# A two-block transformer kernel: the expert weights loaded in runs of 8 KB

## Chip, cores, metric

One core of one Trainium2 chip. The metric is device time of one execution in microseconds (us). Before the change three runs took 3195.36, 3199.36 and 3201.74 us.

## What is computed

Two blocks follow each other on a sequence of 512 tokens with 1024 features, all in float32. The first (depth 2) mixes tokens with gated linear attention and differential attention and then has a mixture of 32 experts; the second (depth 2) has grouped attention, spatial gating, a convolution and a gated feed-forward. The change lies in the mixture of experts of the first block, cut to what matters:

```python
for l in range(DEPTH):                         # 2
    mod = c_act @ w_ada[l] + b_ada[l]
    sh1, sc1, g1, sh2, sc2, g2 = jnp.split(mod, 6, axis=-1)
    ...
    h = rms_norm(x, norm2_g[l]) * (1.0 + sc2[:, None, :]) + sh2[:, None, :]
    # hier_moe: every token goes to 2 of the 32 experts, with gates
    hu = lax.ragged_dot(xs, w1, sizes)         # w1: [32, 1024, 1024]
    h_gate, h_up = jnp.split(hu, 2, axis=-1)
    ys = lax.ragged_dot(jax.nn.silu(h_gate) * h_up, w2, sizes)   # w2: [32, 512, 1024]
    out = jnp.zeros_like(t).at[tok_s].add(ys * gate)
    x = x + g2[:, None, :] * out
```

A contraction is a sum over rows of the weight matrix; it may run over them in any order, if both factors use the same one.

## The kernel before

The program is written by hand: five instruction streams (SyncE loads weights, GpSimd does small loads, indirect transfers and subtractions, TensorE, VectorE, ScalarE), tied by semaphores. For each layer of the first block there is a stage A (norm, projections, both attentions, router) and an expert stage; then the second block follows. Tiles, rings and waits of stage A come from a table that lists them in order (`order_a`); SyncE issues the loads in the order of `blocks_a`.

**Expert stage.** Every expert has a block of 64 slots for tokens, full or not. For each expert the three matrices of 512 x 1024 (two halves of w1, j = 0 and 1, and w2, j = 2) come from memory, 6 MB in all. Three sets of buffers (w = 0, 1, 2) take them in turn. `expert` (L685) waits for each matrix until TensorE has read the one before in that buffer (`m_set_read`), then issues two loads of 1 MB (L698), each with two chunks k of 128 rows: partition p gets row 128 k + p, so a partition receives two separate rows of 1024 elements (4 KB each).

GpSimd gathers the tokens of an expert (`gather`, L957): partition 64 c + s holds half c (512 features) of the token in slot s. TensorE turns the four 128-column parts (`turn_x`, L1418), and ScalarE (`copy_x`, L2683) copies each half out of PSUM with a scale and a shift per feature: the modulation, whose columns are the bias and scale operands. Then `gate_up` (L1425) multiplies, accumulating over k and j; ScalarE and VectorE make silu times up; `down` (L1442) turns the result (two transposes), multiplies with w2; ScalarE scales by the gate, and GpSimd scatters the rows to `ys_scratch` (`scatter`, L966). TensorE's order per expert is: gate and up of u, turn of the tokens of u + 1, indices of u + 2, down of u. VectorE writes the indices for a scatter (L2123) only when the scatter before has landed; ScalarE and TensorE are behind that. There are 31 experts in a loop unrolled in rounds, and then single blocks for what did not fit.

**Modulation.** In stage A twelve small blocks of `w_ada` make mod in PSUM, which is added up in `T[:, 0]` (`add_ada`). `turn_ada(1, 11)` (L1129, called at L1339 in step 16 of the attention loop of 18 steps) transposes the later two thirds of it into the PSUM tile ("adt", 1), and VectorE's `modulation` (L1829) adds the bias: `mod` has feature 128 k + p in column k of partition p, and `s1[:, 8:16]` (L2007) is (1 + scale) times the norm's gain. The biases and gains come from `prow`, whose rows are parts of 128 features. `link` (L1798) makes VectorE wait for its own last result.

## Time and profile before

| | |
|---|---|
| median of 3 runs | 3199.36 us (3195.36 to 3201.74) |
| profiled execution | 3193.79 us, span 3191.9 us |
| TensorE busy | 2934.5 us, 92% |
| VectorE, ScalarE, GpSimd busy | 1281.3, 1082.1, 1046.2 us |
| moved by the DMA engines | 665.98 MB, mean 209 GB/s |
| expert loads of 1 MB, both layers | 390 (180 + 90 + 60 + 40 + 20 in the table of issues) |
| packets of the hardware queue | 280128, none of 8 KB or more |
| chain that ended last | TensorE 62%, SyncE's queue 21%, DMA 5%, VectorE 4% |

Time runs from the start of the span. The expert stage of layer 0 lies at about 500 to 1000 us, that of layer 1 at about 1490 to 1990 us; stage A lies before each, and the second block takes the rest. A DMA share is the part of the time in which the 16 DMA engines moved packets. "PE" is TensorE, "PEld" its weight loads, "DVE" VectorE, "ACT" ScalarE, "POOL" GpSimd, "SPq" SyncE's queue.

### The profile page before, as it was taken

The page shows a single profiled execution, that of the slowest core. Times are in us where ns is not written, and L with a number is a line of the kernel's source. Part 1 is how long each engine was busy: PE and PEld are TensorE (multiplying, and loading weights), DVE is VectorE, ACT ScalarE, POOL GpSimd, SP SyncE. Part 2 cuts the span into 40 slices and gives each one's busy share as a digit, 9 for nine tenths or more (in the row PEclk, how much of TensorE's full clock was granted, in tenths as well). Part 3 has the DMA queues.
Part 4 walks back from the last instruction along what each step waited for, and adds up shares of the span by engine and source line. Part 5 has one row for each costly group of instructions (what it writes and reads, how often), then busy time and mean ns, then how long its engine had stood idle before and what let it go on. Part 6 is the DMA issues. An engine that isn't in the chain of part 4 may idle for free.

```text
span 3191.9 us, 43608 instructions
## 1 busy us (share of the span) xinstructions
PE 2934.5 (92%) x15073; PEld 1937.7 (61%) x15073; DVE 1281.3 (40%) x2094; ACT 1082.1 (34%) x1796; POOL 1046.2 (33%) x917
## 2 busy tenths in 40 slices
PE   8999997888887999997998787899999999999999
PEld 5776783333224776685333222666888776688877
DVE  5575433111114565633111111445676223557631
ACT  4435422222223335522222221454433233543330
POOL 6322441111112432350111111514554542245543
PEclk8999998999998999998999999999999999999999
DMA  6335349999998324437999999311323241132232
GB/s 244 132 113 179 129 165 363 409 408 409 408 407 332 132 91 164 165 122 304 406 408 409 410 407 381 118 54 53 106 84 84 73 131 52 53 106 85 74 106 66
DMA packets 295224, 665.98 MB, mean 209 GB/s; under 512 B 24043, under 2 KB 118696, under 8 KB 295056
## 3 DMA queue, kind: packets, MB, share of 16 engines
q1 hardware_dynamic: 280128, 638.13, 53.6%
q0 software_dynamic: 14928, 25.63, 2.3%
q8 instruction: 104, 1.70, 0.2%
q14 instruction: 64, 0.52, 0.1%
HBM read 647.89 MB, written 33.03 MB: 213 GB/s over the span
## 4 chain that ended last, share of the span: by engine, by line
PE 62%; SPq 21%; DMA 5%; DVE 4%; issue 4%; ACT 2%; POOL 1%; ACTq 0%; DVEq 0%; POOLq 0%
PE psum L1039 60%; SPq L698 20%; DMA ys_scratch<-s_units,s_put_at 2%; DMA s_ring<-in_w_expert_in 1%; POOL s_parts L905 1%; PE psum L1681 1%; ACT s_parts L2460 1%; DMA h_scratch<-s_units 1%; DVE s_hid_low L2430 1%; PE psum L1297 1%; SPq L718 1%; DMA s_ring<-in_w_in 0%; ACT s_units L2460 0%; ACT s_units L2702 0%; DMA s_units<-h_scratch,s_take_at 0%
## 5 line engine op out<-in xcount | busy, mean ns | idle before, releaser
L1009 POOL TENSOR_TENSOR s_parts<-s_ring,s_parts 128x512 fp32r<-128x512 f32 x368 | 511.6, 1425 | 638.6 <-ACT s_parts L2460 638.6
L1039 PE MATMUL psum<-s_hid_low,s_parts 128*128 128x512 f32 x2752 | 642.6, 390 | 3.7 <-DVE s_hid_low L2430 3.7
L1039 PE MATMUL psum<-s_parts 128*128 128x512 f32 x2320 | 595.1, 403 | 7.5 <-ACT s_parts L2460 3.9
L1039 PEld LDWEIGHTS psum<-s_hid_low,s_parts 128*128 128x128 f32 x2752 | 515.6, 188 | 115.2 <-DVE s_hid_low L2430 7.1
L1039 PE MATMUL psum<-s_ring,s_units 128*64 128x512 f32 x2160 | 511.6, 622 | 63.4 <-DMA s_ring<-in_w_expert_in 35.2
L1039 PEld LDWEIGHTS psum<-s_parts 128*128 128x128 f32 x2320 | 434.7, 190 | 121.5 <-issue 20.2
L905 POOL TENSOR_TENSOR s_parts<-s_ring,s_parts 128x512 fp32r<-128x512 f32 x224 | 302.1, 1384 | 480.3 <-ACT s_parts L2460 480.3
L1039 PE MATMUL psum<-s_units 128*128 (+8 forms) x2056 | 375.9, 441 | 82.0 <-DVE s_gsl L2124 42.6
L1039 PEld LDWEIGHTS psum<-s_ring,s_units 128*64 128x64 f32 x2160 | 152.9, 142 | 386.2 <-issue 290.4
L1039 PEld LDWEIGHTS psum<-s_units 64*128 64x128 f32 (+3 forms) x2056 | 185.4, 174 | 239.8 <-issue 188.7
L2460 ACT ACTIVATE s_parts<-s_ring 128x4096 fp32r<-128x4096 f32 (+2 forms) x80 | 265.7, 3322 | 171.1 <-PE psum L1039 100.5
L1039 PE MATMUL psum<-s_h_low,s_parts 128*128 128x512 f32 x1152 | 293.9, 390 | 0.0
L957 POOL DMA_INDIRECT s_units<-h_scratch,s_take_at x67 | 80.3, 1198 | 644.0 <-DVE s_take_at L2118 613.7
L2123 DVE TENSOR_SCALAR s_put_at<-psum,s_half_row 128x1 int32<-128x1 f32 x62 | 13.5, 218 | 656.7 <-DMA ys_scratch<-s_units,s_put_at 656.7
L1039 PEld LDWEIGHTS psum<-s_h_low,s_parts 128*128 128x128 f32 x1152 | 216.1, 188 | 46.3 <-issue 1.0
L2688 ACT ACTIVATE s_units<-psum,s_mod,s_s 128x64 f32<-128x64 f32 x536 | 165.9, 416 | 39.3 <-PE psum L1422 33.3
L2460 ACT ACTIVATE s_units<-psum 128x512 f32<-128x512 f32 (+1 forms) x168 | 98.3, 603 | 200.0 <-PE psum L1039 189.9
L2866 ACT ACTIVATE s_units<-s_temps,s_par 128x512 f32<-128x512 f32 x88 | 63.6, 723 | 297.4 <-DVE s_temps L2436 297.0
L2695 ACT ACTIVATE s_units<-psum 128x256 f32<-128x256 f32 x65 | 25.0, 384 | 411.1 <-PE psum L1039 411.0
L966 POOL DMA_INDIRECT ys_scratch<-s_units,s_put_at x62 | 63.0, 1017 | 286.7 <-ACT s_units L2702 249.3
L2702 ACT ACTIVATE s_units<-psum,s_gsl 128x512 f32<-128x512 f32 x65 | 44.7, 688 | 264.8 <-PE psum L1039 264.8
L2440 DVE SCALAR_TENSOR_TENSOR s_units<-s_temps,s_par,s_units 128x511 f32<-128x511 f32 x88 | 91.2, 1036 | 74.7 <-ACT s_units L2866 74.7
(426 smaller groups left out, 2958.0 us busy)
## 6 DMA issues: line engine op xcount, KB each, us to landing
s_ring<-in_w_expert_in SPq DMA_DIRECT2D x180, 1024.0 KB, 19.1
s_ring<-in_w_expert_out SPq DMA_DIRECT2D x90, 1024.0 KB, 19.1
s_units<-in_w_expert_in SPq DMA_DIRECT2D x60, 1024.0 KB, 19.4
s_ring<-in_w_in SPq DMA_DIRECT2D x28, 2048.0 KB, 9.2
s_ring<-in_w_ada SPq DMA_DIRECT2D x24, 2048.0 KB, 9.0
s_hT<-in_w_expert_out SPq DMA_DIRECT2D x40, 1024.0 KB, 19.2
s_ring<-in_ffn_w_up SPq DMA_DIRECT2D x40, 1024.0 KB, 6.7
s_ring<-in_ffn_w_down SPq DMA_DIRECT2D x16, 1408.0 KB, 7.0
```

What stands on the lines that cost most here:

```text
L698: sp.dma_start(set_piece(w, j, c), matrix[:, first + 2 * c:first + 2 * c + 2, :]).then_inc(weights_in_m[w][j][c], 16)
L718: sp.dma_start(slot_view(s, k, n), src).then_inc(weights_in_a[s], 16)
L905: ins = pool.tensor_tensor(parts[:, s, cols], ring[:, s, cols], high_of(n)[:, cols].bitcast(F32), ALU.subtract)
L957: pool.indirect_dma_start(out=xs[u % 2], out_offset=None, in_=h2_dram[:, :], in_offset=bass.IndirectOffsetOnAxis(ap=take_at[:, u % 2, 0:1] ...
L966: pool.indirect_dma_start(out=ys_dram[:, :], out_offset=bass.IndirectOffsetOnAxis(ap=put_at[:, u, 0:1], axis=0), in_=ys[u], in_offset=None ...
L1009: ins = pool.tensor_tensor(parts[:, s, cols], ring[:, s, cols], parts[:, 4 + n % 2, cols].bitcast(F32), ALU.subtract)
L1039: return pe.matmul(o, lhsT=lhsT, rhs=rhs, start=start, stop=stop)
L2440: link(ve.scalar_tensor_tensor(out=up_t[:, b, 1:SEQ], in0=o[:, 0:SEQ - 1], scalar=w[0], in1=up_t[:, b, 1:SEQ], op0=ALU.mult, op1=ALU.add))
L2460: return ae.activation(o, i, ACT.Copy) if scale is None else ae.activation(o, i, ACT.Copy, scale=scale)
L2688: ins = ae.activation(xsT[u % 2][:, k, CAP * j:CAP * j + CAP], psum[:, 2, slots], ACT.Identity, bias=mod[:, 24 + f:25 + f], scale=s1[:, 8 ...
L2702: ae.activation(ys[b], psum[:, 5 + b, :], ACT.Copy, scale=gsl[:, b:b + 1]).then_inc(m_ys_made.sem, m_ys_made.more())
L2866: ae.activation(up_t[:, n % 4, :], product[n % 2], ACT.Copy, scale=par[:, col:col + 1]).then_inc(up_centre.sem, up_centre.more())
```

## The change

A load still has two chunks of 128 rows, but the row of chunk k = 2 q + b in partition p is now 256 q + 2 p + b: the two rows of a partition are neighbours in memory and make one run of 8 KB. What meets the weights in the contraction follows: the transposes read every second column, and shift and scale are also made in that order, in a new tile `paired`, by eight small matmuls per layer on TensorE and some small operations on VectorE. The slot number of the single blocks moves into a free column.

```diff
-LINKS = {"A": 178, "B": 81}
+LINKS = {"A": 181, "B": 81}
...
-    slot_token = sb("slot_token", [P, 1])
+    paired = sb("paired", [P, 6, 2, 2])
+    shift_of_pairs, scale_of_pairs = (paired[:, a:a + 2].rearrange("p m q b -> p (m q b)") for a in (0, 2))
...
+    slot_token = U[:, 26, 0:1]
...
-                matrix = kn(inp["w_expert_in" if j < 2 else "w_expert_out"][l, e], 0, D)
-                first = 4 * j if j < 2 else 0
+                matrix = inp["w_expert_in" if j < 2 else "w_expert_out"][l, e].rearrange("(q p b) n -> p q b n", p=P, b=2)
+                first = 2 * j if j < 2 else 0
                 for c in range(2):
-                    sp.dma_start(set_piece(w, j, c), matrix[:, first + 2 * c:first + 2 * c + 2, :]).then_inc(weights_in_m[w][j][c], 16)
+                    sp.dma_start(set_piece(w, j, c), matrix[:, first + c]).then_inc(weights_in_m[w][j][c], 16)
...
                 pe.wait_ge(TA.by(("ada", last)).sem, TA.freed_at(l, ("ada", last)))
+                if half:
+                    for h in range(2):
+                        for b in range(2):
+                            mm(o[64 * h:64 * h + 64, P + P * b:2 * P + P * b], T[:, 0, 0:P].rearrange("p (i b) -> p b i", b=2)[:, b, :], ident[:], True, True)
+                            mm(o[64 * h:64 * h + 64, 384 + 64 * b:448 + 64 * b], prow[0:64, 0, :].rearrange("p (i b) -> p b i", b=2)[:, b, :], ident[0:64, 0:64], True, True)
                 done(pe.transpose(o[:, 0:P], T[:, 0, 0:P], ident[:]))
...
                 for k in range(4):
-                    last = pe.transpose(psum[:, 2, tok(k)], xs[u % 2][:, tok(k)], ident[:])
+                    last = pe.transpose(psum[:, 2, tok(k)], xs[u % 2][:, 256 * (k // 2):256 * (k // 2) + 256].rearrange("p (i b) -> p b i", b=2)[:, k % 2, :], ident[:])
...
                 for k in range(2):
-                    last = pe.transpose(psum[:, 4, tok(k)], act[b][:, tok(k)], ident[:])
+                    last = pe.transpose(psum[:, 4, tok(k)], act[b].rearrange("p (i c) -> p c i", c=2)[:, k, :], ident[:])
...
                 if i == LAST_STEP - 1:
+                    o = done(("adt", 1))
+                    for h in range(2):
+                        half = slice(64 * h, 64 * h + 64)
+                        rows_of = o[half, 384:512].rearrange("p (b m r) -> p m r b", b=2, r=4)
+                        for q in range(2):
+                            ve.tensor_copy(paired[half, 0:4, q, :], rows_of[:, 6:10, 2 * q + h, :])
+                            ins = ve.tensor_copy(paired[half, 4:6, q, :], rows_of[:, 14:16, 2 * q + h, :])
+                    link(ins)
+                    for h in range(2):
+                        half = slice(64 * h, 64 * h + 64)
+                        made_of = o[half, P:384].rearrange("p (b r j) -> p r j b", b=2, r=4)
+                        for q in range(2):
+                            ins = ve.tensor_tensor(paired[half, 0:4, q, :], made_of[:, 2 * q + h, 6:10, :], paired[half, 0:4, q, :], ALU.add)
+                    link(ins)
+                    link(ve.scalar_tensor_tensor(out=scale_of_pairs, in0=scale_of_pairs, scalar=1.0, in1=paired[:, 4:6].rearrange("p m q b -> p (m q b)"), op0=ALU.add, op1=ALU.mult))
                     modulation(1, 4, 12)
...
                         ins = ae.activation(xsT[u % 2][:, k, CAP * j:CAP * j + CAP], psum[:, 2, slots], ACT.Identity,
-                                            bias=mod[:, 24 + f:25 + f], scale=s1[:, 8 + f:9 + f])
+                                            bias=shift_of_pairs[:, f:f + 1], scale=scale_of_pairs[:, f:f + 1])
```

The order of instructions shows two places. SyncE's loads for one matrix of the first set that is loaded, before:

```order
L698 ISA
L698 DMA s_units<-in_w_expert_in 128x2x1024
L698 ISA
L698 DMA s_units<-in_w_expert_in 128x2x1024
```

and now:

```order
L700 ISA
L700 DMA s_units<-in_w_expert_in 128x2048
L700 ISA
L700 DMA s_units<-in_w_expert_in 128x2048
```

Number and place of the loads are as before; the instruction's pattern has one run per partition.

TensorE at the second turn of the modulation (`s_temps` is T, `s_prow` the rows of parameters), before:

```order
L1039 MATMUL psum<-s_hid_low,s_parts 128x512 x4
L1083 REGISTER_ALU
L1132 REGISTER_ALU
L1133 MATMUL psum<-s_ident,s_temps 128x128
L1083 REGISTER_ALU
L1297 MATMUL psum<-s_ident,s_units 128x128 x4
```

and now:

```order
L1041 MATMUL psum<-s_hid_low,s_parts 128x512 x4
L1085 REGISTER_ALU
L1134 REGISTER_ALU
L1041 MATMUL psum<-s_ident,s_temps 64x128
L1041 MATMUL psum<-s_ident,s_prow 64x64
L1041 MATMUL psum<-s_ident,s_temps 64x128
L1041 MATMUL psum<-s_ident,s_prow 64x64
L1041 MATMUL psum<-s_ident,s_temps 64x128
L1041 MATMUL psum<-s_ident,s_prow 64x64
L1041 MATMUL psum<-s_ident,s_temps 64x128
L1041 MATMUL psum<-s_ident,s_prow 64x64
L1140 MATMUL psum<-s_ident,s_temps 128x128
```

Eight small matmuls stand ahead of the transpose, behind the same waits. VectorE has 13 more instructions behind the tile's signal, ahead of L1831 of before.

## Rows read from the trace of the kernel before

**Rows 1.** page, part 2: 40 slices of about 80 us
```profile
GB/s 244 132 113 179 129 165 363 409 408 409 408 407 332 132 91 164 165 122 304 406 408 409 410 407 381 118 54 53 106 84 84 73 131 52 53 106 85 74 106 66
```

**Rows 2.** busy time by windows, in us; the loads at the start, then both expert stages
```profile
core 0: us, PE busy (x) PEld busy (x) DVE busy (x) ACT busy (x) POOL busy (x), PEclk, DMA share, GB/s
4.00:6.00 2.00, 1.09 (x5) 1.09 (x6) 0.00 (x0) 0.00 (x0) 1.65 (x7) 1.00 1.03 408
14.00:20.00 6.00, 6.00 (x9) 2.36 (x8) 0.00 (x0) 2.33 (x3) 3.95 (x34) 0.57 1.05 387
520.00:560.00 40.00, 35.75 (x182) 14.02 (x178) 5.03 (x18) 10.64 (x30) 5.58 (x5) 1.00 1.03 405
560.00:960.00 400.00, 345.30 (x1636) 129.05 (x1632) 48.98 (x156) 97.66 (x265) 58.71 (x53) 0.97 1.03 408
1500.00:1560.00 60.00, 54.27 (x271) 20.99 (x271) 8.50 (x26) 16.12 (x47) 10.01 (x9) 1.00 1.03 406
1560.00:1950.00 390.00, 330.27 (x1572) 122.68 (x1568) 46.70 (x151) 93.70 (x255) 57.10 (x51) 0.97 1.03 408
```

**Rows 3.** SyncE's queue in time, start and length, expert stage of layer 0
```profile
642.41 12.94 SPq L698 DMA_DIRECT2D s_ring<-in_w_expert_in  x4
```

**Rows 4.** DMA queues and issues, 560 to 960 us; median us to landing
```profile
q1 hardware_dynamic: 40392, 155.71, 97.6%
q0 software_dynamic: 4217, 7.45, 5.0%
...
s_ring<-in_w_expert_in SPq DMA_DIRECT2D x66, 1024.0 KB, 19.3
```

**Rows 5.** chain that ended last, 515 to 560 us: start, length
```profile
523.69 5.90 DMA ys_scratch<-s_units,s_put_at
...
537.55 5.93 DMA ys_scratch<-s_units,s_put_at
...
551.38 5.85 DMA ys_scratch<-s_units,s_put_at
```

**Rows 6.** L966, the scatter, expert stage of layer 0, then of layer 1
```profile
L966 POOL DMA_INDIRECT ys_scratch<-s_units,s_put_at x31: 1002/1017/1038, 523.7 to 976.3; - x31
...
L966 POOL DMA_INDIRECT ys_scratch<-s_units,s_put_at x31: 1002/1014/1030, 1506.3 to 1959.9; - x31
```

**Rows 7.** small GpSimd loads, us to landing: first 60 us, then 440 to 520 us
```profile
s_prow<-in_diff_qnorm_g POOLq DMA_DIRECT2D x2, 0.2 KB, 5.0
...
s_prow<-in_diff_qnorm_g POOLq DMA_DIRECT2D x2, 0.2 KB, 1.7
...
s_prow<-in_q_norm_g POOLq DMA_DIRECT2D x2, 0.2 KB, 5.2
```

**Rows 8.** TensorE in time around the second turn of the modulation, layer 0
```profile
342.78 0.62 PE L1039 MATMUL psum<-s_ring,s_cact 128*32 128x128 f32 x16
...
346.59 0.27 PE L1133 MATMUL psum<-s_ident,s_temps 128*128 128x128 f32 x1
346.70 0.60 PE L1297 MATMUL psum<-s_ident,s_units 128*128 128x128 f32 x4
```

**Rows 9.** chain that ended last, 340 to 395 us
```profile
346.75 0.11 PE psum L1133
...
347.30 47.78 PE psum L1039 x196
```

**Rows 10.** VectorE in time at the same place
```profile
347.39 0.18 DVE L1831 TENSOR_TENSOR s_mod<-psum,s_par 128x32 f32<-128x32 f32 x1
347.61 0.17 DVE L2007 SCALAR_TENSOR_TENSOR s_s<-s_mod,s_par 128x8 f32<-128x8 f32 x1
350.09 0.69 DVE L1973 TENSOR_TENSOR s_temps<-psum,s_temps 128x512 f32<-128x512 f32 x1 [2.31 <-PE psum L1039]
```

**Rows 11.** groups by line and form, 560 to 960 us: the transposes of an expert
```profile
L1422 PE MATMUL psum<-s_ident,s_units 128*128 128x128 f32 x104 | 17.1, 287 | 0.0
...
L1447 PE MATMUL psum<-s_ident,s_units 128*128 128x128 f32 x52 | 11.1, 295 | 1.1 <-DVE s_units L2181 1.1
```

More of the change, by code:

```diff
@@ L2130, in write_gate @@
                     ve.wait_ge(m_scattered[1], count * 16 + 32)
-                ve.tensor_copy(slot_token[:], psum[:, 7, 0:1]).then_inc(m_put_written.sem, m_put_written.more())
+                ve.tensor_copy(slot_token, psum[:, 7, 0:1]).then_inc(m_put_written.sem, m_put_written.more())
                 ve.tensor_copy(gsl[:, 1:2], psum[:, 7, 2:3]).then_inc(m_put_written.sem, m_put_written.more())
```

## Prediction

> **What bounds the kernel.** I read the 40 slices first, then windows, then the chain of waits. In the slices [rows 1] the transfer rate stands at 406 to 410 GB/s in two blocks of about 450 us, the expert stages of the two layers, and far below that elsewhere. The windows [rows 2] show the same rate with the 16 DMA engines busy at a share of 1.03 (a share over 1 means that records overlap a little), while TensorE is busy for 345 of 400 us and the other engines for less than a quarter. SyncE's queue has the next set's buffers free and still needs 12.94 us to issue four 1 MB loads [rows 3]: it is held by the full DMA queue. A load lands 19.3 us after its issue [rows 4], although 1 MB takes 2.6 us at 408 GB/s. So from about 520 us and from about 1500 us the DMA engines set the pace.
>
> The chain names something else in the first part of the stage: one scatter after the other, 13.86 us apart, each 5.9 us in flight [rows 5]. That is the speed of the computing side. But the 31 scatters of a stage span 452.6 and 453.6 us [rows 6], 15.1 us apiece. The three weight sets loaded ahead are eaten up first, and then the loads decide. Between the two lie 1.2 us per expert: what a faster transfer can win before the computing side binds.
>
> **The change, part by part.**
>
> *Loads.* Bytes, number of DMAs and buffers stay. The instruction moves rows of 2048 elements instead of 2 x 1024. If the queue turns each into one packet, a load has 128 packets of 8 KB and not 256 of 4 KB. What a packet costs beyond its bytes comes from two saturated windows [rows 2]. At 14 to 20 us the adaptation weights come in runs of 512 elements, 2 KB, at 387 GB/s: 16 x 2048 / 387 = 84.7 ns per packet and engine. In the expert stage, with 4 KB, 408 GB/s give 16 x 4096 / 408 = 160.6 ns. Two small packets less one large one leave 8.8 ns per packet. (The input rows at 4 to 6 us, 4 KB too, also reach 408.) An 8 KB packet should then take 2 x 160.6 - 8.8 = 312.4 ns, or 420 GB/s.
> The queue of these loads moved 155.71 MB in 400 us [rows 4]. Over the 890 us of saturated windows [rows 2] (520 to 960, 1500 to 1950) that is 346 MB, or 346e6 / 16 / 8192 = 2640 pairs per engine. 2640 x 8.8 ns = **23.3 us** less. The first loads of each layer, before 520 us, win nothing: they wait for buffers and for the router. No row has an HBM load of 8 KB from this queue, so the price is bounded: at the low end 0 (no fixed part is saved), at the high end half as much again, 13 ns, 34 us. I take the middle, since two loads from the same queue give it.
>
> *Landing of the small transfers.* Gathers and scatters share the engines with packets twice as long. The nearest rows are tiny GpSimd loads [rows 7]: 1.7 us to landing on an idle queue, 5.0 us behind the 2 KB packets of the first 60 us, 5.2 us for the similar ones issued last, behind the first expert loads of 4 KB. Twice the packet, hardly more wait: what they wait behind is an amount of bytes, not a number of packets. So the scatter's 6 us stay within 0.3 us, and I count 0. The Trainium skill ("DMA: Bandwidth & Descriptors", Queues, rings and completion order) says otherwise: an engine drains a whole packet of about 9 to 17 descriptors from one ring before it turns to the next. By that rule the wait would double with the descriptor; rows 7 do not agree, as it did not double from 2 to 4 KB.
>
> *Transposes.* Four of the input and two of the activation per expert now read every second column. Contiguous ones take 287 and 295 ns [rows 11]. No row has such a stride, so: 0 at the low end, twice the time, 6 x 0.29 = 1.7 us per expert, at the high end. A gain is excluded, as the element count is the same. I take 0, for two reasons: TensorE is not what is waited for after the first experts, and only more than the margin of the computing side (below) could show.
> The Trainium skill ("SBUF — State Buffer", Door 1: The DMA port swizzle) states that accesses keep full bandwidth as long as two fall into one 16-byte line; a stride of two fp32 does just that. No row here shows it, and the sum does not use it.
>
> *TensorE, once per layer.* Eight small matmuls stand before the turn of the modulation, at 346.6 us [rows 8]. TensorE is the chain there and goes on unbroken for 47.78 us [rows 9], so they count in full. Neighbours: 16 matmuls with 128 moving columns in 0.62 us, 0.04 us each; four transposes in 0.60 us, 0.15 us each; a single one 0.27 us [rows 8]. The new ones alternate between two kinds and fill half the array; 8 x 0.15 = 1.2 us, 0.3 to 2.2 us as ends. Two layers: **+2.4 us** (0.6 to 4.4).
>
> *VectorE, once per layer.* Eight copies, four additions, one product, with three waits on its own results. The nearest small ones take 0.18 and 0.17 us, 0.22 us apart [rows 10]; 13 x 0.2 = 2.6 us. Behind them VectorE was idle for 2.31 us, until TensorE's next tile [rows 10], which now comes 1.2 us later. At most 0.3 us of delay is left, and TensorE's run of 47.78 us waits for none of it: 0. Without that cover it would be 2 x 2.6 us. ScalarE reads bias and scale from another tile in the same 8 instructions, and the slot number has another place: 0.
>
> **Sum:** -23.3 + 2.4 = -20.9 us. The profiled execution took 3193.8 us (span 3191.9) and would take 3172.9. It lies 0.17% under the median of the three runs, 3199.4, and against that the forecast is **3178.5 us**, 0.65% less. Its own range runs from -34 + 0.6 to -16 + 4.4: 3166 to 3188 us.
>
> **Rivals.**
> *The computing side takes over (slower).* Twice the packet length could double the wait of a scatter in the engines. Its place is the scatter's landing, which VectorE awaits before it writes the next indices; its own products, TensorE's down part and the next scatter are queued behind that. The price is the loaded part of the flight: 6.0 less the 3 us or so that a transfer needs on its own (1.7 us landing plus 1.0 us of issue in rows 6), so +3 us per expert: 13.86 + 3 = 16.9 us. After the change the loads would need 15.1 - 23.3 / 60 = 14.7 us per expert; so from 0.8 us more on the computing side decides, from 1.2 us more the kernel is slower. At 16.9 us, 60 intervals x 1.8 us: about +108 us, with the 2.4 us 3310 us. The rule of the Trainium skill quoted above would show in this way. For it: 13.86 us is near 15.1, and the chain does run through the scatters. Against it: rows 7. The transposes at their high end would work the same way, 13.86 + 1.7 = 15.6, +0.5 x 60 + 2.4: 3232 us. Together 9%.
> *The rate does not move (the change doesn't do what it says).* The queue may cut at 4 KB, or the 408 GB/s may be a limit of memory or ports that small packets miss for another reason. Only the additions stay: 3199.4 + 2.4 = 3202 us, 0.08% more. For it: every packet of these loads is 4 KB so far, and nothing shows a longer one from this queue. Against it: the rate does depend on the run (387 to 408). 15%.
> *Half the gain.* The rate rises but the computing side, 0.8 us away, meets it in part: 3188 to 3193 us. 6%, in the range.
>
> **Numbers.** Forecast 70%, half the gain 6%, no movement 15%, slower by the computing side 9%. A difference within 0.2% (6.4 us) can't be told from none. Faster: 0.76; same: 0.15; slower: 0.09. The range reaches from the forecast's low end to the case without movement: 3166 to 3202 us.
>
> **What would show it.** Right: packets of the loads' queue fall by 390 x 128 = 49920 (390 expert loads in the profile's table); the windows of the expert stages read 418 to 421 GB/s; 31 scatters span about 441 us; landing of a scatter stays at 6.0 us; the turn of the modulation is some 1.2 us longer on TensorE. SyncE's loads may take longer to land, as more bytes fit into the queue; that alone costs nothing. Wrong: 408 GB/s as before (cut packets or another limit), a share below 1 in the windows with scatters over 7 us in flight (computing side), or transposes at 0.5 us.

## The result and the profile after

The changed kernel takes **3266.76 us** (median of 4 runs, 3253.45 to 3270.57) against 3200.55 us for the kernel before on the same chip (3195.36 to 3203.01, 4 runs): ratio 1.0206, 95% interval [1.0188, 1.0223]. It is 2.1% slower; the forecast was 0.65% faster. The profiled execution took 3270.2 us, span 3268.4. Two of the four runs of rest_4k below (3357.86 and 3369.13 us) fell in a slower state, over 1.5% above the fastest of the same kernel, and are left out of its time.

Line numbers of after are those of before plus 2 (SyncE's loads L700, matmuls L1041, scatter L968), further down plus 7 (turn of the tokens L1429, of the activation L1454) and more (put index L2145, gate column L2146). The 40 slices and the queues of the page:

```profile
PEclk8999997889899999998899899999999999999999
GB/s 238 129 115 189 107 187 354 400 401 402 398 403 260 156 64 161 187 106 264 389 402 391 405 403 289 215 60 52 104 97 58 107 121 59 52 84 97 78 99 69
...
q1 hardware_dynamic: 230208, 638.13, 51.7%
```

The packets fell by 280128 - 230208 = 49920, exactly as forecast, so the chip does use single packets of 8 KB. But the blocks of the expert stages read 389 to 405 GB/s instead of 406 to 410 [rows 1] and last longer. The windows of both stages, to be laid beside [rows 2]:

```profile
560.00:960.00 400.00, 344.05 (x1520) 133.61 (x1518) 45.65 (x144) 90.33 (x245) 53.62 (x49) 0.90 0.98 400
1560.00:1950.00 390.00, 334.36 (x1466) 128.85 (x1468) 44.90 (x140) 86.86 (x236) 52.68 (x48) 0.90 0.98 397
```

TensorE is busy as long as before (344 of 400 us) and gets less done (1520 matmuls, before 1636), since its granted clock is 0.90 instead of 0.97. The DMA share fell from 1.03 to 0.98: the engines are no longer full. The queue says the same. A load lands 8.8 us after its issue, not 19.3 [rows 4], and SyncE's queue is 1% of the chain that ended last, not 21%; TensorE is 70% of it. So **the computing side sets the pace**. Landings in the window 560 to 960 us:

```profile
s_ring<-in_w_expert_in SPq DMA_DIRECT2D x66, 1024.0 KB, 8.8
...
ys_scratch<-s_units,s_put_at POOLq DMA_INDIRECT x25, 6.9
s_units<-h_scratch,s_take_at POOLq DMA_INDIRECT x24, 6.7
```

Before, the scatter took 6.1 us in the same window and the gather 6.3:

```profile
s_units<-h_scratch,s_take_at POOLq DMA_INDIRECT x27, 6.3
ys_scratch<-s_units,s_put_at POOLq DMA_INDIRECT x26, 6.1
```

The same scatters in rows like [rows 6]:

```profile
L968 POOL DMA_INDIRECT ys_scratch<-s_units,s_put_at x31: 1002/1017/1038, 531.6 to 1018.3; - x31
...
L968 POOL DMA_INDIRECT ys_scratch<-s_units,s_put_at x31: 1001/1014/1030, 1552.0 to 2041.1; - x31
```

486.7 and 489.1 us, where before had 452.6 and 453.6: +34.1 and +35.5 us, or 16.2 and 16.3 us per expert for 15.1. That is 69.6 of the 76.5 us by which the spans differ. The rest: the first scatter comes 7.9 us later, the way from the last scatter of layer 0 to the first of layer 1 takes 533.7 us for 530.0, and what follows the last scatter is 4.7 us shorter.

Groups by line and form, 560 to 960 us, show where TensorE stands still and what the new access costs. First the matmuls that make the indices (name of the engine and line, then shapes, count | busy, mean ns | idle before, releaser), then the two kinds of transposes with their weight loads:

```profile
L1041 PE MATMUL psum<-s_units 128*128 x192 | 26.4, 260 | 43.3 <-DVE s_gsl L2146 43.3
...
L1429 PE MATMUL psum<-s_ident,s_units 128*128 128x128 f32 x96 | 17.9, 309 | 0.0
L1429 PEld LDWEIGHTS psum<-s_ident,s_units 128*128 128x128 f32 x96 | 13.3, 207 | 19.5 <-issue 19.5
L1454 PE MATMUL psum<-s_ident,s_units 128*128 128x128 f32 x48 | 11.7, 329 | 0.0
L1454 PEld LDWEIGHTS psum<-s_ident,s_units 128*128 128x128 f32 x48 | 9.5, 247 | 0.0
```

The same groups of before, window as above:

```profile
L1039 PE MATMUL psum<-s_units 128*128 x208 | 26.6, 251 | 20.3 <-DVE s_gsl L2124 20.3
...
L1422 PEld LDWEIGHTS psum<-s_ident,s_units 128*128 128x128 f32 x104 | 10.9, 141 | 21.1 <-issue 21.1
...
L1447 PEld LDWEIGHTS psum<-s_ident,s_units 128*128 128x128 f32 x52 | 7.2, 179 | 1.2 <-DVE s_units L2181 1.2
```

Eight index matmuls belong to an expert, so TensorE waited 43.3 / 24 = 1.8 us per expert for VectorE, which waited for the scatter to land; before it was 20.3 / 26 = 0.8 us. What such a wait does to the clock is seen in windows of 2 us. Here 664 to 676 us of after, first TensorE's two pauses in time (in square brackets: idle before, releaser), then the windows:

```profile
668.50 1.05 PE L1041 MATMUL psum<-s_units 128*128 x8 [2.16 <-DVE s_gsl L2146]
...
670.41 4.06 PE L1041 MATMUL psum<-s_ring,s_units 128*64 128x512 f32 x10 [0.54 <-DVE s_units L2207]
```

```profile
664.00:666.00 2.00, 2.00 (x11) 0.69 (x8) 0.00 (x0) 0.21 (x1) 0.00 (x0) 1.00 1.01 397
666.00:668.00 2.00, 0.34 (x3) 0.15 (x2) 0.00 (x0) 1.80 (x7) 0.00 (x0) 1.00 1.05 440
668.00:670.00 2.00, 1.37 (x10) 1.19 (x10) 0.80 (x5) 0.85 (x3) 0.00 (x0) 1.00 0.96 406
670.00:672.00 2.00, 1.59 (x4) 0.51 (x6) 1.05 (x3) 0.00 (x0) 1.10 (x1) 0.62 1.06 446
672.00:674.00 2.00, 2.00 (x8) 0.64 (x6) 0.00 (x0) 0.00 (x0) 0.24 (x1) 0.53 0.98 414
674.00:676.00 2.00, 2.00 (x12) 0.60 (x10) 0.00 (x0) 0.02 (x1) 0.00 (x0) 1.00 1.01 422
```

TensorE stood still for much of 666 to 670 us; from about 670.5 to 674 it works at half its clock (1.2 of 2.4 GHz) and has 8 large matmuls in 2 us instead of 11 or 12. The half clock begins some 2 us behind the end of the pause for the indices, just behind the second, short pause. That short pause of about 0.5 us ahead of the down part is there in the trace of before too, and in the runs with filler matmuls below, whose clock is 1.00; the long one is what differs. The trace's clock record has 23 such stretches between the first and last scatter of each layer, 89 and 92 us together; before had 8 and 6 (27 and 20 us). An interval between scatters without one takes 14.2 to 14.7 us in layer 0 (the last 12.8), one with it mostly 16 to 17.5. Half the clock for 3.9 us (89 / 23) costs 1.9 us of work, so 23 stretches in 30 intervals cost 1.5 us per expert: an estimate from these figures, and the size of the step from 14.7 to 16.2 us.

Theory A, with which the experiments began (the first expectations call it the packet theory): 8 KB packets make the scatter land later, the longer wait for the scatter takes TensorE's clock down, and the low clock is most of the loss. Its rivals: the strided transposes, the 8 KB packets by themselves, or the order in which the engines wait.

### The profile page after: what moved, and what is told of

Same layout as the page of the kernel before. It is cut to its first block, busy times and chain, and to the rows that moved or that the text cites. A ratio compares the mean times of both kernels' runs of the same rounds, so it can differ in the third digit from the quotient of the medians.

```text
span 3268.4 us, 43706 instructions
## 1 busy us (share of the span) xinstructions
PE 3006.2 (92%) x15105; PEld 1977.7 (61%) x15105; DVE 1286.7 (39%) x2120; ACT 1081.1 (33%) x1796; POOL 1045.6 (32%) x917
## 3 DMA queue, kind: packets, MB, share of 16 engines
q1 hardware_dynamic: 230208, 638.13, 51.7%
## 4 chain that ended last, share of the span: by engine, by line
PE 70%; DMA 14%; DVE 5%; issue 5%; ACT 3%; POOL 1%; SPq 1%; DVEq 0%; ACTq 0%; POOLq 0%
PE psum L1041 68%; DMA ys_scratch<-s_units,s_put_at 12%; ACT s_units L2724 1%; POOL s_parts L907 1%; PE psum L1688 1%; DVE s_units L2207 1%; ACT s_parts L2482 1%; DMA h_scratch<-s_units 1%; DVE s_hid_low L2452 1%; PE psum L1304 1%; SPq L720 1%; PE psum L1454 0%; DMA s_ring<-in_w_in 0%; ACT s_units L2482 0%; DVE s_h_low L1856 0%
## 5 line engine op out<-in xcount | busy, mean ns | idle before, releaser
L1041 PE MATMUL psum<-s_hid_low,s_parts 128*128 128x512 f32 x2752 | 642.7, 390 | 3.7 <-DVE s_hid_low L2452 3.7
L1041 PE MATMUL psum<-s_parts 128*128 128x512 f32 x2320 | 595.9, 404 | 7.5 <-ACT s_parts L2482 3.9
L1041 PEld LDWEIGHTS psum<-s_hid_low,s_parts 128*128 128x128 f32 x2752 | 515.7, 188 | 115.1 <-DVE s_hid_low L2452 7.1
L1041 PE MATMUL psum<-s_ring,s_units 128*64 128x512 f32 x2160 | 541.5, 659 | 27.1 <-DVE s_units L2207 23.7
L1041 PEld LDWEIGHTS psum<-s_parts 128*128 128x128 f32 x2320 | 435.3, 191 | 121.3 <-issue 18.1
L1041 PE MATMUL psum<-s_units 128*128 (+8 forms) x2056 | 375.2, 441 | 126.0 <-DVE s_gsl L2146 106.0
L1041 PEld LDWEIGHTS psum<-s_ring,s_units 128*64 128x64 f32 x2160 | 165.0, 151 | 367.5 <-issue 333.8
L1041 PEld LDWEIGHTS psum<-s_units 64*128 64x128 f32 (+3 forms) x2056 | 188.4, 176 | 279.4 <-issue 253.7
L2145 DVE TENSOR_SCALAR s_put_at<-psum,s_half_row 128x1 int32<-128x1 f32 x62 | 13.5, 218 | 766.6 <-DMA ys_scratch<-s_units,s_put_at 766.6
L1041 PE MATMUL psum<-s_h_low,s_parts 128*128 128x512 f32 x1152 | 293.9, 390 | 0.0
L1041 PEld LDWEIGHTS psum<-s_h_low,s_parts 128*128 128x128 f32 x1152 | 216.2, 188 | 46.0 <-issue 1.0
L2710 ACT ACTIVATE s_units<-psum,s_paired 128x64 f32<-128x64 f32 x536 | 165.4, 415 | 43.5 <-PE psum L1429 42.8
L968 POOL DMA_INDIRECT ys_scratch<-s_units,s_put_at x62 | 63.0, 1017 | 345.3 <-ACT s_units L2724 300.6
```

The source lines that it names most:

```text
L968: pool.indirect_dma_start(out=ys_dram[:, :], out_offset=bass.IndirectOffsetOnAxis(ap=put_at[:, u, 0:1], axis=0), in_=ys[u], in_offset=None ...
L1041: return pe.matmul(o, lhsT=lhsT, rhs=rhs, start=start, stop=stop)
L2710: ins = ae.activation(xsT[u % 2][:, k, CAP * j:CAP * j + CAP], psum[:, 2, slots], ACT.Identity, bias=shift_of_pairs[:, f:f + 1], scale=sca ...
```

## The experiments

All were timed in 3 or 5 rounds beside the kernel before on the same chip (medians of 3195 to 3198 us), and the ratios are to that; the row "after" is the result above, to its 3200.55 us. The factors, one by one:

| run | packets | transposes | added | median us | ratio [95%] | layer 0: 31 scatters, us; clock, GB/s 560:960 |
|---|---|---|---|---|---|---|
| before | 4 KB | contiguous | - | 3195 to 3198 | 1 | 452.6; 0.97, 408 |
| after | 8 KB | strided | - | 3266.76 | 1.0206 [1.0188, 1.0223] | 486.7; 0.90, 400 |
| strided_4k | 4 KB | strided | - | 3179.60 | 0.9949 [0.9932, 0.9966] | 452.4; 0.96, 408 |
| loads_8k | 8 KB | contiguous | - | 3226.49 | 1.0101 [1.0074, 1.0128] | 485.7; 0.92, 405 |
| fill_8k | 8 KB | strided | 8 matmuls | 3186.98 | 0.9957 [0.9937, 0.9977] | 444.1; 1.00, 419 |
| fill_8k_again | 8 KB | strided | 8 matmuls | 3190.06 | 0.9975 [0.9962, 0.9988] | 443.0; 1.00, 420 |
| fill_loads_8k | 8 KB | contiguous | 8 matmuls | 3148.61 | 0.9849 [0.983, 0.9867] | 440.9; 1.00, 420 |
| fill_4k | 4 KB | contiguous | 8 matmuls | 3199.81 | 1.0015 [1.0003, 1.0026] | 451.9; 1.00, 408 |
| delay_4k_b | 4 KB | contiguous | 6 copies | 3201.75 | 1.0016 [1.0002, 1.003] | 454.2; 0.94, 408 |
| delay12_4k | 4 KB | contiguous | 12 copies | 3256.17 | 1.0171 [1.0145, 1.0196] | 486.7; 0.91, 401 |

strided_4k, loads_8k and fill_loads_8k multiply columns with the wrong rows. The second layer then routes otherwise and moves 659.7 MB in all, not 666.0, which is one expert's 6.3 MB or about 15 us at 408 GB/s. Their whole times are lower by that, so they are compared in layer 0.

### Which part does it

**rest_4k**: the change with 4 KB packets; load c takes row b = c of both q, so that the rows a load reads lie 8 KB apart in memory, and TensorE needs the second load of a matrix before its second chunk and not before its third.

```diff
-                    sp.dma_start(set_piece(w, j, c), matrix[:, first + c]).then_inc(weights_in_m[w][j][c], 16)
+                    sp.dma_start(set_piece(w, j, c), matrix[:, first:first + 2, c]).then_inc(weights_in_m[w][j][c], 16)
...
-                        if k % 2 == 0:
-                            pe.wait_ge(weights_in_m[w][j][k // 2], used * 16 + 16)
+                        if k < 2:
+                            pe.wait_ge(weights_in_m[w][j][k], used * 16 + 16)
...
```

> All of the change but the packet: each load takes one row of each pair, 4 KB, from two blocks of 256 rows; strided transposes, the added matmuls and VectorE operations stay. Packet theory (8 KB packets hold up the scatters, TensorE then waits longer and its clock falls once per expert): the slowdown goes, 3203 to 3212 us (3200.6 plus 2 x 2.7 us of additions in stage A), scatters 15.1 to 15.3 us apart, landing 6.0 us, granted clock of the expert stage 0.97. Stride theory (the transposes that read every second column cost the computing side its margin): stays at 3240 to 3270 us.

Measured: 3269.65 and 3286.60 us, no better than the change itself and, by the number alone, where the stride theory had it. Layer 0 kept 15.2 us per expert (408 GB/s, clock 0.92), layer 1 took 17.3 us (378 GB/s, clock 0.89). In layer 1, 1560 to 1950 us, the scatter lands latest of all runs, with 4 KB packets:

```profile
ys_scratch<-s_units,s_put_at POOLq DMA_INDIRECT x22, 7.7
```

```profile
L1041 PE MATMUL psum<-s_units 128*128 x184 | 25.9, 263 | 57.9 <-DVE s_gsl L2146 57.9
```

That is 57.9 / 23 = 2.5 us of wait per expert and 29 half-clock stretches in 30 intervals. The chain that ended last runs there through the scatter (46% of 1640 to 1740 us), and TensorE's only waits from 1560 to 1950 us are these 57.9 us and 11.6 us for VectorE ahead of the down part, none for weights. So this run agrees with the second half of theory A, in that the late scatter goes with a long wait and a low clock; but the size of a packet is not all that makes a scatter late. What did it here (the order of the rows in memory is one candidate) was not tested. The run does not answer its own question, so the stride needed strided_4k below.

**loads_8k**: only the load's pattern of the diff, transposes and the rest as before.

> The reverse: the kernel before with loads of 8 KB runs alone; transposes and modulation stay in the old order, so weights meet the wrong columns, and the routing of layer 1 may differ (layer 0's does not). Packet theory: slow, layer 0's 31 scatters some 16.0 to 16.5 us apart, landing 6.9 us, clock near 0.90; in all 3240 to 3265 us. Stride theory: fast, 3177 to 3190 us, scatters 14.7 us apart.

Measured, layer 0:

```profile
L966 POOL DMA_INDIRECT ys_scratch<-s_units,s_put_at x31: 1003/1021/1042, 529.4 to 1015.1; - x31
```

485.7 us for 31 scatters, as slow as the change (486.7), at a clock of 0.92, with 47.6 us of wait before the indices and the scatter landing after 6.9 us. **In layer 0 the 8 KB packets alone cause the loss.** In layer 1, which routes otherwise here, the same loads took 463.9 us, with 16 half-clock stretches and a landing of 6.6 us: slower than before too, by less.

**strided_4k**: the change with the loads and waits of before, word for word.

```diff
-                matrix = inp["w_expert_in" if j < 2 else "w_expert_out"][l, e].rearrange("(q p b) n -> p q b n", p=P, b=2)
-                first = 2 * j if j < 2 else 0
+                matrix = kn(inp["w_expert_in" if j < 2 else "w_expert_out"][l, e], 0, D)
+                first = 4 * j if j < 2 else 0
                 for c in range(2):
-                    sp.dma_start(set_piece(w, j, c), matrix[:, first + c]).then_inc(weights_in_m[w][j][c], 16)
+                    sp.dma_start(set_piece(w, j, c), matrix[:, first + 2 * c:first + 2 * c + 2, :]).then_inc(weights_in_m[w][j][c], 16)
```

> The change with the loads of before, word for word: 4 KB packets of neighbouring rows, and the waits of before, with strided transposes, paired shift and scale and the additions of the first stage. It leaves out that weights and columns agree, so it multiplies wrong pairs; the second layer routes by them, so only the first layer's expert stage is compared. Theory A (a matmul that reads every second column, 22 and 34 ns longer and with weight loads of 207 and 247 in place of 141 and 179 ns, costs the clock by itself): window 560:960 at a clock of 0.90 to 0.93, scatters over 15.6 us apart, 3215 to 3270 us. Theory C (the clock was lost in the earlier 4 KB run through its waiting for both pieces): clock 0.97, scatters 15.1 us apart, 3205 us (3195 plus 5.4 for the additions, plus or minus 5).

Measured: as theory C expected of the stride. The stage takes 452.4 us (before 452.6) at 408 GB/s, though the transposes are those that take longer:

```profile
L1429 PE MATMUL psum<-s_ident,s_units 128*128 128x128 f32 x108 | 20.1, 308 | 0.0
...
L1454 PE MATMUL psum<-s_ident,s_units 128*128 128x128 f32 x54 | 12.9, 323 | 1.0 <-DVE s_units L2203 1.0
```

The stride costs 21 ns and 28 ns per transpose [rows 11], some 0.15 us per expert, hidden under the loads. There are 11 and 10 half-clock stretches where before had 8 and 6. Theory C's reason for the slow rest_4k, its waits for both loads, is not borne out: its trace shows the late scatter above.

### Is it the clock

**fill_8k**, and **fill_8k_again**: the changed kernel with eight idle matmuls where TensorE would wait for the indices; their output is read by nobody.

```diff
+                    for _ in range(8):
+                        mm(psum[:, 3, 0:P], ident[:], ident[:], True, True)
                     indices(number + ROUND * g, ROUND * g + (u + 2), u + 2)
```

> The changed kernel with 8 idle matmuls of 128 columns per expert into an unused PSUM bank, placed where TensorE waits for the scatter's landing (between the turn of the tokens and the indices). If the falling clock is a part of the loss: clock back to 0.95 or more in the expert stage, scatters 14.8 to 15.3 us apart, 3185 to 3225 us. If the clock only follows and the late landing alone costs the time: no gain, 3260 to 3290 us, as TensorE's work only grows by about 1.2 us per expert.

> The changed kernel with the same eight idle matmuls once more, beside the one with 4 KB packets. Theory A: again 0.3 to 0.6% faster than before, 3178 to 3192 us, 418 GB/s in the expert stage, scatters 14.8 to 15.1 us apart, and faster than the 4 KB version with eight matmuls. Theory B: equal to that version.

Measured: 3186.98 and 3190.06 us, faster than before both times, if by less than half a per cent. The windows of fill_8k_again:

```profile
560.00:960.00 400.00, 385.15 (x2120) 185.63 (x2118) 50.44 (x161) 100.96 (x275) 59.09 (x55) 1.00 1.01 420
1560.00:1950.00 390.00, 372.99 (x2038) 179.06 (x2038) 50.77 (x161) 99.17 (x272) 57.33 (x52) 0.99 1.01 419
```

and TensorE in time in fill_8k, 652.8 to 657 us (the eight stand as 16 records, in two passes, and take 1.95 us):

```profile
652.79 0.74 PE L1429 MATMUL psum<-s_ident,s_units 128*128 128x128 f32 x4
653.37 1.95 PE L1041 MATMUL psum<-s_ident 128*128 128x128 f32 x16
655.16 1.05 PE L1041 MATMUL psum<-s_units 128*128 x8
```

The long pause is gone, the clock is at 1.00, and the 8 KB packets deliver the 420 GB/s that the prediction had worked out. TensorE does more work and the kernel is 77 to 80 us faster than the change. The cure is not complete in every trace: in layer 1 of fill_8k four half-clock stretches (17 us) remain, and the 31 scatters take 453.1 us there, as before the change. The Trainium skill ("TensorE: Matmul & The Clock Gate", A second HAM failure mode: psum-queue depth-cycling) tells of a kernel in which short pauses between groups of matmuls make the clock oscillate. The trace of after agrees: in layer 0 the pauses ahead of its half-clock stretches are 1.15 to 2.9 us long.

**fill_4k**: the kernel before with the same eight.

> The kernel before, 4 KB packets and contiguous transposes, with eight idle 128-column matmuls ahead of the indices of each expert. It separates what the eight matmuls give from what the 8 KB packets give. Theory A (the matmuls only mend a clock that the changed kernel had lost; before, the queue of the loads set the pace at a granted clock of 0.97): the DMA share stays 1.03 at 408 GB/s in the window 560:960, the 31 scatters stay 15.1 us apart, time 3195 +- 4 us, no difference. Theory B (the matmuls help any version by the same amount, and the 8 KB packets give nothing): scatters 14.8 us apart, about 3183 us, as much as the changed kernel with the same eight.

Measured: 451.9 us for the stage, 408 GB/s, clock 1.00, 3199.81 us, ratio 1.0015: theory A, 0.8 us above its range. A full clock gives nothing where the loads set the pace; the gain of fill_8k is that of the packets.

**fill_loads_8k**: loads_8k with the eight.

> The kernel before with 8 KB packets alone, contiguous transposes and no additions, and eight idle matmuls ahead of the indices. It multiplies wrong pairs, so only the first layer's expert stage is compared. Theory A (with the clock kept up, 8 KB packets give what the packet count says and the stride costs little): clock 0.98 or more, 418 to 420 GB/s, scatters 14.7 to 14.9 us apart, as in the changed kernel with eight matmuls (14.80). Theory D (the stride still costs 0.3 us or more per expert when the clock is kept up): scatters 0.3 us or more closer than 14.80.

Measured: 14.7 us per expert in both layers, 420 and 417 GB/s. With strided transposes layer 0 took 14.8 (443.0 and 444.1 us for 440.9), so the stride costs about 0.1 us per expert here, not 0.3: theory A.

**reorder_8k**: down(u) ahead of the indices of u + 2 on TensorE, the activation's product ahead of the indices on VectorE, scatter ahead of gather on GpSimd.

```diff
-                    indices(number + ROUND * g, ROUND * g + (u + 2), u + 2)
                     down(made + ROUND * g, used[w] + (2 * g + u // SETS), u, w)
+                    indices(number + ROUND * g, ROUND * g + (u + 2), u + 2)
...
-                    write_put(number + 2 * g, counts[1 - u] + (g + u), u + 1)
                     multiply(made + 2 * g, u)
-                    write_take(number + 2 * g, taken[u] + g, u + 2)
                     turned_act(made + 2 * g, u)
+                    write_put(number + 2 * g, counts[1 - u] + (g + u), u + 1)
+                    write_take(number + 2 * g, taken[u] + g, u + 2)
...
-                    gather(number + 2 * g, u + 2)
                     scatter(made + 2 * g, number + 2 * g, u)
+                    gather(number + 2 * g, u + 2)
```

> The changed kernel with the wait for the scatter taken out of TensorE's way: TensorE does the down part of an expert before the indices of the one after next, VectorE writes the indices for the scatter after its two products, and GpSimd issues the scatter before the gather. Packet theory: the scatter has 4 us more to land, the computing side needs about 14 us per expert and the loads decide at 420 GB/s: 3180 to 3200 us, clock 0.95 or more. Stride theory: little changes, as the transposes are still there: 3240 us or more.

Measured: 3289.13 us, ratio 1.029 [1.0269, 1.0312], clock 0.91. A miss: the wait went away before the indices and came back before the tokens, longer (52.1 / 24 = 2.2 us per expert):

```profile
L1041 PE MATMUL psum<-s_units 128*128 x199 | 26.3, 255 | 0.0
...
L1429 PE MATMUL psum<-s_ident,s_units 128*128 128x128 f32 x96 | 21.1, 353 | 52.1 <-DMA s_units<-h_scratch,s_take_at 52.1
```

### Is a wait enough, without 8 KB packets

**delay_4k_b**: the kernel before with six one-column copies on VectorE behind the scatter's landing; **delay12_4k** with twelve (the scratch columns of half width).

```diff
                 ve.wait_ge(m_scattered[u % 2], count * 16 + 32)
+                for i in range(6):
+                    ve.tensor_copy(spare[:, u % 2, i:i + 1], psum[:, 7, 1:2])
                 ve.tensor_scalar(put_at[:, u % 2, :], psum[:, 7, 1:2], 2.0, half_row[:, 0:1], ALU.mult, ALU.add).then_inc(m_put_written.sem, m_put_written.more())
```

> The kernel before, word for word in its loads and transposes, with six one-column copies on VectorE between the scatter's landing and the next put indices, about 6 x 0.14 = 0.85 us per expert: as much as the scatter's landing grew with 8 KB packets. Theory A (TensorE's wait for the indices, when it grows by nearly a microsecond, takes the granted clock down, and that is most of the loss): computing side at 13.86 + 0.85 = 14.7 us before the clock answers, then over 15.6 us between scatters, clock 0.90 to 0.93 in the window 560:960, DMA share under 1.0, 3225 to 3265 us, without a single 8 KB packet. Theory E (8 KB packets lower the clock or slow the kernel in another way, a wait alone does not): 14.7 us is under the loads' pace of 15.1 us, so scatters stay 15.1 us apart at 0.97 and the time 3197 +- 4 us.

Measured: between the theories. Wait and clock moved as A says, the time did not:

```profile
L1040 PE MATMUL psum<-s_units 128*128 x215 | 28.8, 257 | 37.0 <-DVE s_gsl L2127 37.0
```

```profile
560.00:960.00 400.00, 348.13 (x1629) 133.52 (x1630) 58.63 (x314) 97.91 (x268) 58.34 (x53) 0.94 1.03 408
```

1.4 us of wait per expert (37.0 / 27), 13 stretches at half clock in a layer; the intervals alternate between about 14.2 and 16.0 us and average 15.1, which is what the loads need anyway. The kernel had slack for nearly half of its experts at the low clock. What A had missed is this slack. The delay was also smaller than meant. VectorE in time, for this run and for the one with twelve:

```profile
650.26 0.49 DVE L2125 COPY s_spare<-psum 128x1 f32<-128x1 f32 x6 [12.91 <-DMA ys_scratch<-s_units,s_put_at]
650.66 0.21 DVE L2126 TENSOR_SCALAR s_put_at<-psum,s_half_row 128x1 int32<-128x1 f32 x1
```

```profile
645.39 0.88 DVE L2125 CAST s_spare<-psum 128x1 bf16<-128x1 f32 x12 [10.65 <-DMA ys_scratch<-s_units,s_put_at]
646.18 0.21 DVE L2126 TENSOR_SCALAR s_put_at<-psum,s_half_row 128x1 int32<-128x1 f32 x1
```

Six copies put the next operation off by 0.40 us and twelve by 0.79 us, a copy every 0.07 us and not every 0.14. So it is the run with twelve that has the delay of the change, whose scatter lands 0.8 us later than before (6.9 for 6.1).

> The kernel before with twelve one-column copies on VectorE between the scatter's landing and the next put indices, twice the last delay: about 1.7 us per expert, computing side 13.86 + 0.2 (the rest of what six copies cost in the first intervals, 14.1) + 0.3 to 0.85 us = 14.4 to 14.9 us with the clock kept up, still under the loads' 15.1. Theory A (the length of the wait before the indices sets how often the clock falls): wait over 1.8 us per expert, clock 0.90 to 0.92 in the window 560:960, scatters over 16 us apart, DMA share under 1.0, 3245 to 3290 us, like the changed kernel, all with 4 KB packets. Theory F (the 8 KB packets take the clock down beyond what their delay does): clock 0.93 to 0.95 and scatters 15.1 to 15.5 us apart, under 3220 us.

Measured: 3256.17 us. All of the changed kernel's picture, with 4 KB packets only:

```profile
L1040 PE MATMUL psum<-s_units 128*128 x192 | 26.8, 263 | 46.9 <-DVE s_gsl L2127 46.9
```

```profile
560.00:960.00 400.00, 338.72 (x1518) 128.20 (x1514) 62.73 (x432) 91.13 (x249) 53.96 (x49) 0.91 1.02 401
```

The wait is 2.0 us per expert, the half-clock stretches are 23 and 23, and the stage of layer 0 takes 486.7 us, by chance to the tenth as in the change (layer 1: 486.6 for 489.1). The scatter itself lands after 6.2 us, as with 4 KB packets elsewhere. **A delay of 0.8 us between the scatter's landing and the indices is enough, and it is the size of the delay in the change.**

**delay_fill_4k_b**: six copies and eight idle matmuls.

> The same six copies together with the eight idle matmuls. Theory A: the matmuls stand where TensorE waits for the indices, so the clock comes back to 0.98 or more, the scatters to 15.1 us, 408 GB/s, 3196 to 3204 us, as the version with eight matmuls and no delay (3199.81). If the loss came from the delay as such and not from the clock: as slow as the run with the delay alone.

Measured: 3196.04 us, ratio 0.9998 [0.9988, 1.0008], clock 1.00, 408 GB/s, no stretch at half clock: theory A. As six copies had cost almost no time, this run shows the clock coming back and not a loss undone; twelve copies with eight matmuls were not run, so that the loss goes when the clock is kept up rests on fill_8k and fill_8k_again.

### How much must be filled, and what packets do

**fill_4_8k_b** and **fill_6_8k**: four or six idle matmuls in place of eight.

> The changed kernel with four idle matmuls in place of eight. Eight end about when the indices may be written, four leave about 0.4 us more of the wait open. Theory A: the clock is between the changed kernel's 0.90 and the 1.00 with eight, nearer to 1.00: 0.96 to 1.00 in the window 560:960, scatters 14.6 to 15.2 us apart, 3180 to 3205 us. If even a few tenths of a microsecond of open wait cost the clock, 0.92 and over 3220 us.

> The changed kernel with six idle matmuls. Four left 26.6 us of wait before the indices in 24 experts (1.1 us each) and the clock at 0.92; eight left 0.3 us and 1.00. Theory A says the clock needs the wait gone: between, 0.94 to 0.99 in the window 560:960, scatters 14.9 to 15.8 us apart, 3190 to 3235 us. If six already close the wait, then 1.00, 14.5 to 14.8 us, and 3175 to 3190 us, the best version; if it is all or nothing, 0.92 and 3245 us.

Measured: with four 3249.29 us, ratio 1.0157 [1.0141, 1.0173]; with six 3195.86 us, 1.0013 [0.9989, 1.0036]. Idle before the indices:

```profile
L1041 PE MATMUL psum<-s_units 128*128 x192 | 25.8, 257 | 26.6 <-DVE s_gsl L2148 26.6
```

```profile
L1041 PE MATMUL psum<-s_units 128*128 x216 | 28.3, 254 | 5.7 <-DVE s_gsl L2148 5.2
```

Four leave 1.1 us per expert and a clock of 0.92, six 0.2 us and 0.97, eight none and 1.00. The expectation for four was a miss: it had 0.4 us more wait open than with eight and not 1.1, since a matmul of these takes 0.24 us (1.95 / 8) and not the 0.1 us that it implies. Note that four leave hardly more wait than the kernel before had (0.8 us), with 21 half-clock stretches in layer 0 against 8; the mean wait alone does not fix how often the clock falls. Nor does a single pause: in delay_4k_b pauses of 1.2 to 1.7 us stand ahead of half-clock stretches and also where none follows. What else decides was not found.

**loads_2k_b**: the kernel before with each load cut into two of half the columns, 2 KB packets.

```diff
-                    sp.dma_start(set_piece(w, j, c), matrix[:, first + 2 * c:first + 2 * c + 2, :]).then_inc(weights_in_m[w][j][c], 16)
+                    for h in range(2):
+                        cols = slice(512 * h, 512 * h + 512)
+                        sp.dma_start(set_piece(w, j, c)[:, :, cols], matrix[:, first + 2 * c:first + 2 * c + 2, cols]).then_inc(weights_in_m[w][j][c], 16)
```

> The kernel before with each 1 MB load issued as two of 0.5 MB that take half the columns: packets of 2 KB, double in number, the same bytes. Two points: the cost of a packet beyond its bytes and the landing of a scatter. By the prediction's two rows 2 KB go at 387 GB/s: the expert windows read 385 to 390 GB/s, scatters 15.8 to 16.0 us apart, 3240 to 3255 us. If a scatter waits for whole packets ahead of it, its landing falls by half of what it rose from 4 to 8 KB (6.0 to 6.6-6.9 us): 5.5 to 5.8 us; if it waits for an amount of bytes it stays 6.0 and the rise at 8 KB needs another cause.

Measured: 3246.92 us, ratio 1.0159 [1.014, 1.0177], 386 GB/s, 15.9 us per expert, all as expected. So the rate by packet size is 386, 408 and 420 GB/s for 2, 4 and 8 KB. The scatter lands after 5.9 (here), 6.0 (fill_4k; 6.1 in before) and 6.6 us (fill_8k_again), with a DMA share above 1 in all of them. Both expectations on the landing miss in part: from 2 to 4 KB it is flat, from 4 to 8 KB it rises.

## Why the prediction was wrong

- **Loads, -23.3 us: right as a price, and not collected.** Packets fell by 49920; the 8.8 ns per packet gave 420 GB/s, and fill_8k_again and fill_loads_8k read 420 in layer 0 and 419 and 417 in layer 1. The best measure is layer 0 of fill_loads_8k, 11.7 us less than before (440.9 for 452.6), half of 23.3. In the change the loads do not set the pace. With the clock kept up the two stages won 9.6 and 7.1 us (fill_8k_again: 443.0 and 446.5 us of 452.6 and 453.6), 16.7 us in all; in fill_8k 8.5 and 0.5 us. In the range, the -16 us at the cautious end is worked out nowhere: the text bounds this term by 0.
- **"Landing of the small transfers ... I count 0": the first step that failed.** The scatter's landing went from 6.0 to 6.6 us beside full queues and from 6.1 to 6.9 us in the window of the change. Rows 7 compared 2 with 4 KB, and there it is indeed flat (5.9 and 6.0 us). The conclusion that it "is an amount of bytes" was carried to 8 KB, where it does not hold: +0.6 to +0.8 us. The rival's +3 us was too large. The Trainium skill's rule ("DMA: Bandwidth & Descriptors", Queues, rings and completion order), as the prediction read it, has the wait grow with the descriptor: the sign is right from 4 to 8 KB, the size is not, and from 2 to 4 KB the runs show no growth. Why the landing rises stays open, and rest_4k (7.7 us with 4 KB packets in layer 1) shows that packet size is not the whole of it.
- **"From 0.8 us more on the computing side decides": the margin was right, its use was not. This is the second step that failed, and the larger.** 13.86 + 0.8 = 14.7 us is just what the loads would need: by that sum a draw, and the gain of the packets kept. The sum held the computing side's pace for fixed, as read from [rows 5] at full clock. It isn't: when TensorE waits nearly 2 us instead of 0.8, its clock stands at half for 3.9 us in three experts of four (23 of 30), and the mean interval goes to 16.2. No rival had a clock in it, though the 0.97 in [rows 2] was there to be asked about. This term, about 1.5 us x 60 = 90 us, is the loss: the 70 us of the two stages and the 23 us of gain that were not collected.
- **Transposes, 0:** measured 309 and 329 ns for 287 and 295; near the low end of the bounds (0.15 to 0.2 of 1.7 us). Their weight loads grew more, from 141 and 179 to 207 and 247 ns, so the full bandwidth that the prediction quoted for this stride is not what the rows show. Hidden in strided_4k; in layer 0 loads_8k and the change differ by 1.0 us. In the sum the 0 was good; only the range left the high bound out.
- **TensorE, once per layer, 1.2 us:** measured from 350.47 to 352.98 us in the trace of after, 2.5 us, above the upper bound of 2.2. That place is reached at 350.5 us and in the trace of before at 346.6 [rows 8], so 3.9 of the 7.9 us by which the first scatter comes later lie ahead of the first added matmul, where nothing was changed on TensorE; the first scatter comes at 529.9 us in fill_4k, too, which has no additions in stage A:

```profile
350.47 0.44 PE L1041 MATMUL psum<-s_ident,s_temps 128*64 128x128 f32 x2
350.84 0.33 PE L1041 MATMUL psum<-s_ident,s_prow 64*64 64x64 f32 x2
...
352.98 0.33 PE L1140 MATMUL psum<-s_ident,s_temps 128*128 128x128 f32 x1
```

  Each pair of small matmuls of two kinds takes 0.63 us (2.51 / 4); the neighbours from which they were priced have one shape and don't change it.
- **VectorE, 0: right.** Its 13 operations run from 353.34 to 354.87 us, and it then waits again for TensorE:

```profile
354.70 0.17 DVE L2027 SCALAR_TENSOR_TENSOR s_paired<-s_paired 128x8 f32<-128x8 f32 x1
...
356.55 0.69 DVE L1980 TENSOR_TENSOR s_temps<-psum,s_temps 128x512 f32<-128x512 f32 x1 [1.25 <-PE psum L1041]
```

- **The rival "computing side takes over"** is what happened (a share of 0.98, scatters near 7 us in flight), with a loss of 66 us, not 108 (3266.76 for 3200.55), and a mechanism of which only the first half was written down. It had 9%.

## What to carry to other kernels

When two sides of a pipeline are within a few per cent, price a change on both, and ask of TensorE's side at which granted clock its pace was read and what a longer pause would make of it. The larger DMA packet bought rate here (420 GB/s for 408) and lengthened the small transfers beside it (the scatter by 0.6 to 0.8 us, the gather by 0.4); if a small one is on the computing side's loop, look for the pause that it opens. Where such a pause can't be removed, matmuls of no use that fill it can keep the clock: here eight per expert turned +2.1% into -0.25 to -0.43%, while too few (four) left +1.6%.

## What the runs showed that was not expected

- With pauses of about 2 us, once in 16 us, the mean clock was 0.90, and 1.00 with the pauses filled. The half clock mostly came 2 to 3 us behind the end of the pause.
- A delay with slack cost hardly any time (ratio 1.0016) but did cost clock (0.97 to 0.94 in delay_4k_b), so a falling clock is a warning ahead of a slower kernel.
- The landing of a small indirect transfer beside full queues is 5.9, 6.0 and 6.6 us with neighbours' packets of 2, 4 and 8 KB, but 7.7 us in layer 1 of rest_4k with 4 KB packets from rows that lie 8 KB apart.
- A weight load for a transpose that reads every second column takes 207 ns for 141, and 247 for 179; the matmul itself 309 for 287.
